# Moving 32 more tokens of a product-key expert layer from the dense path to row fetches

## The reference

```python
q = (xt @ w_query).reshape(NT, PEER_HEADS, 2, D_KEY // 2)      # 8 heads
s = jnp.einsum('nhpd,pkd->nhpk', q, sub_keys)                  # 2 x 128 keys
v1, i1 = lax.top_k(s[:, :, 0], 16); v2, i2 = lax.top_k(s[:, :, 1], 16)
cand = (v1[..., :, None] + v2[..., None, :]).reshape(NT, 8, 256)
best, ci = lax.top_k(cand, 16)
idx = e1 * N_KEYS + e2            # 8 x 16 = 128 experts of 16384 for a token
gate = jax.nn.softmax(best, axis=-1)
act = jax.nn.gelu(jnp.einsum('cd,ced->ce', xc, expert_u[ic]), approximate=False)
y = jnp.einsum('ce,ced->cd', gc * act, expert_v[ic])
```

## Time and profile before

| | |
|---|---|
| Runs | 4306.17 us median of 3 (4293.15 to 4307.22) |
| The profiled execution | 4302.8 us, of which its span is 4301.0 |
| PE, DVE, POOL, ACT busy | 4162.1, 2571.1, 2259.6, 1306.7 us |
| DMA | 832.09 MB, mean 193 GB/s |
| Gates, 48 units | from 2320.9 us of the span to 2770.9 |
| Rest, 40 units | to 3129.4 |
| Values, 128 units, and the last norm | to 4301.0 |

### The profile page before, as it was taken

How to read it: one execution, slowest core, us unless ns; L and a number is a source line. 1 busy time by engine, 2 the same in 40 slices (tenths; PEclk the granted TensorE clock), 3 DMA queues, 4 the chain that set the end, 5 groups by cost and what they waited for, 6 DMA issues and landing times.

```text
span 4301.0 us, 69877 instructions
## 1 busy us (share of the span) xinstructions
PE 4162.1 (97%) x27220; PEld 3743.0 (87%) x27220; DVE 2571.1 (60%) x3908; ACT 1306.7 (30%) x1265; POOL 2259.6 (53%) x866
## 2 busy tenths in 40 slices
PE   7999999999999999899999999999988999999998
PEld 5777777777788778799999999999978999999997
DVE  4344343444554542477775999745558777777775
ACT  4332322333322221233233444422222222222223
POOL 4333223233234344344445544567767778888884
PEclk9999999999999999999999999999999999999999
DMA  3222222222223442233334555499979989899983
GB/s 121 89 88 80 86 87 82 84 87 87 97 89 104 140 170 98 80 122 122 123 120 145 191 188 195 186 353 395 380 291 356 356 326 356 351 358 360 357 329 109
DMA packets 205230, 832.09 MB, mean 193 GB/s; under 512 B 15864, under 2 KB 98040, under 8 KB 120080
## 3 DMA queue, kind: packets, MB, share of 16 engines
q1 hardware_dynamic: 135024, 486.69, 31.5%
q0 software_dynamic: 36864, 268.45, 15.1%
q10 hardware_dynamic: 33184, 74.63, 4.5%
HBM read 760.99 MB, written 68.71 MB: 193 GB/s over the span
## 4 chain that ended last, share of the span: by engine, by line
PE 79%; issue 9%; POOL 4%; DVE 3%; DMA 3%; ACT 1%; SPq 0%; POOLq 0%; DVEq 0%; ACTq 0%
PE ps L348 17%; PE ps L350 16%; PE ps L349 16%; PE ps L1874 7%; PE ps L1875 7%; PE ps L1876 7%; POOL wl L343 4%; DMA raw<-stream 2%; PE ps L1578 2%; PE ps L1836 1%; ACT wh L339 1%; DVE rowb L1416 1%; DVE gal L1423 1%; PE ps L1730 0%; PE ps L1721 0%
## 5 line engine op out<-in xcount | busy, mean ns | idle before, releaser
L343 POOL TENSOR_TENSOR wl<-raw,wh 128x2048 fp32r<-128x2048 f32 x396 | 1839.0, 4644 | 1878.5 <-ACT wh L339 1878.0
L348 PE MATMUL ps<-xh,wh 128*128 128x384 f32 (+1 forms) x3904 | 1463.3, 375 | 43.4 <-POOL wl L343 22.2
L350 PE MATMUL ps<-xh,wl 128*128 128x384 f32 (+1 forms) x3904 | 1430.0, 366 | 0.0
L349 PE MATMUL ps<-xl,wh 128*128 128x384 f32 (+1 forms) x3904 | 1429.4, 366 | 0.0
L339 ACT ACTIVATE wh<-raw 128x2048 fp32r<-128x2048 f32 x396 | 759.0, 1917 | 1937.5 <-PE ps L350 1066.2
L348 PEld LDWEIGHTS ps<-xh,wh 128*128 128x128 f32 x3904 | 737.9, 189 | 140.4 <-issue 36.8
L350 PEld LDWEIGHTS ps<-xh,wl 128*128 128x128 f32 x3904 | 737.4, 189 | 83.4
L349 PEld LDWEIGHTS ps<-xl,wh 128*128 128x128 f32 x3904 | 738.1, 189 | 81.3 <-issue 7.7
L1874 PE MATMUL ps<-gah,wh 128*128 128x384 f32 x2048 | 699.7, 342 | 44.4 <-POOL wl L343 22.3
L1875 PE MATMUL ps<-gal,wh 128*128 128x384 f32 x2048 | 696.7, 340 | 0.0
L1876 PE MATMUL ps<-gah,wl 128*128 128x384 f32 x2048 | 696.1, 340 | 0.0
(11 more groups left out here) (321 smaller groups left out, 3700.6 us busy)
## 6 DMA issues: line engine op xcount, KB each, us to landing
raw<-stream SPq DMA_DIRECT2D x396, 1024.0 KB, 4.8
gelu_scratch<-preb ACTq DMA_DIRECT2D x128, 192.0 KB
gates_scratch<-stage ACTq DMA_DIRECT2D x12, 2048.0 KB, 6.5
gt<-gates_scratch SPq DMA_DIRECT2D x32, 768.0 KB
act<-gelu_scratch SPq DMA_DIRECT2D x32, 768.0 KB
mergegate_scratch<-sgb ACTq DMA_DIRECT2D x32, 256.0 KB, 2.1
sgm<-mergegate_scratch SPq DMA_DIRECT2D x32, 256.0 KB, 2.7
h_in<-x_t SPq DMA_DIRECT2D x4, 1024.0 KB, 8.8
```

What stands on the lines that cost most here:

```text
L343: pool.tensor_tensor(wl[s][:, :], raw[s][:, :], wh[s][:, :].bitcast(F32), ALU.subtract).then_inc(w_lo, 1)
L348: pe.matmul(dst, w_h, h[:, kx, lo:], start=start, stop=False)
L349: pe.matmul(dst, w_h, l[:, kx, lo:], start=False, stop=False)
L350: return pe.matmul(dst, w_l, h[:, kx, lo:], start=False, stop=stop)
```

## The change

G becomes 160 and N 352. The 32 new fetched tokens have 128 slots each as well; they are packed four slots to one DMA (32 tokens x 4 slots on 128 partitions), so 32 more fetches of u-rows and 32 of v-rows (`ALL` = 160). Their numbers and gates are brought onto the four quarters of the partitions by eight small DMAs (`idx_1`), their x stands four times in `xd`, and their sum is taken by a matmul with `sel`, which adds the quarters.

The fetches begin in the gates stage, from its fourth unit on: 12 by its twelfth unit, 116 to the third unit of the rest, then the 32 new ones up to group 3; v-rows 128 over groups 4 to 23 (1.6 to a unit) and 32 over groups 25 to 29. Since xg now holds banks 0 to 3 during the gates, these use one bank (6), two tokens at a time. H waits in DRAM (`h_scratch`) from the head routing to the end of the rest; its place holds xd and three row buffers. DVE writes only the plain one-hot (`ohp`), ACT multiplies it by the two gate halves (`act_scale`). The gates are 88 sets of four tokens: two sets with each of 12 score units (`GATES_TWO`), one with each of 64 (`GATES_ONE`); the rest has 12 units. `stage` holds 16 tokens (`GT`) instead of 32, so a group's gates come in pieces of 256 bytes. The group load stands behind the fourth unit's load instead of the second's. The sum of the first 128 tokens is taken after group 24, the other at the end.

```diff
@@ constants
-SC_HEAD, SC_TAIL, SC_EGT, OH = 4, 6, 2, 8
+SC_HEAD, SC_TAIL, SC_EGT, OH = 4, 6, 2, 4
-G = P
+G2 = 32
+SETS = P // G2
+G = P + G2
+ALL = SLOTS + SLOTS // SETS
+GATES_TWO = 12
+GATES_ONE = N // OH - 2 * GATES_TWO
-VALUE_FETCHES = [range(min(N_REST + 2 * k, SLOTS), min(N_REST + 2 * k + 2, SLOTS)) for k in range(V_FIRST)]
+fetches(0, 12, range(3, GATES_TWO), 0)
+fetches(12, SLOTS - 12, range(GATES_TWO, F_GATES + R_TURNED - 1), 0)
...
+fetches(ALL, SLOTS, range(at_group(V_GROUP) - 1, at_group(W_GROUP - 1) - 1), 0)
+fetches(ALL + SLOTS, ALL - SLOTS, range(at_group(W_GROUP) - 2, at_group(GROUPS - 3) + 1), at_group(W_GROUP))
-    GT = 32
+    h_d = dram("h_scratch", (4, P, D))
+    GT = 16
@@ load_values
-                    if c == 1 and ahead:
+                    if c == 3 and ahead:
@@ scalar
+            act.wait_ge(h_ready, KT)
+            for c in range(4):
+                act.dma_start(h_d[c], quarter_h(c)).then_inc(h_moved[c], 16)
+            def act_scale(k, c):
+                act.wait_ge(oh_plain, k + 1)
+                for u in range(OH):
+                    for m, gate in enumerate((gate_h[:, :].bitcast(F32), gate_l[:, :])):
+                        last = act.activation(oh1[:, OH * c + u, m, :], ohp[:, OH * c + u, :], ACT.Copy, scale=gate[:, bass.ds(OH * k + u, 1)])
+                last.then_inc(oh_ready, 1)
+            def act_upper(p, s, q):
+                act.wait_ge(oh_used, p + 1)
+                act.activation(of_tokens(s, q), gate_parts[:, :, 0, :], ACT.Copy).then_inc(dense_upper, 1)
@@ act_gates
-                    for c in range(2):
-                        act.wait_ge(oh_used, 2 * k + c + 1)
-                        act.activation(of_tokens(s, q, c), gate_parts(c)[:, :, 0, :], ACT.Copy).then_inc(dense_upper, 1)
+                        act_upper(2 * k, s, 2 * q)
+                        if not (last and q == GT // OH - 1):
+                            act_scale(k + 1, (q + 1) % 2)
+                        act_upper(2 * k + 1, s, 2 * q + 1)
+                if r == F_REST - 2:
+                    act.wait_ge(row_used, LAST_IN_H + 1)
+                    act.wait_ge(xg_ready, 2)
+                    for c in range(4):
+                        act.dma_start(quarter_h(c), h_d[c]).then_inc(h_moved[c], 16)
@@ vector
-                for u in range(4):
-                    for m, gate in enumerate((gate_h[:, :].bitcast(F32), gate_l[:, :])):
-                        last = dve.tensor_scalar(oh1[:, 4 * c + u, m, :], iota_ps, EGT[:, 0, bass.ds(at + u, 1)],
-                                                 gate[:, bass.ds(at + u, 1)], ALU.is_equal, ALU.mult)
+                dve.tensor_tensor(oh2[:, c:c + OH, :], numbers, spread(1), ALU.is_equal)
+                dve.tensor_tensor(ohp[:, c:c + OH, :], numbers, spread(0), ALU.is_equal).then_inc(oh_plain, 1)
+                for k in range(2 * j, 2 * j + 2) if j < GATES_TWO else range(GATES_TWO + j, GATES_TWO + j + 1):
+                    dense(2 * k)
+                    if k + 1 < N // OH:
+                        onehots(k + 1)
+                    if used and (j >= GATES_TWO or k % 2):
+                        use(used.pop(0))
+                    dense(2 * k + 1)
@@ tensor
+            def gates(k, c, h, first=False):
+                if not first:
+                    pe.wait_ge(dense_saved, 2 * k + h)
+                if h == 0:
+                    pe.wait_ge(oh_ready, k + 1)
+                for u in range(2):
+                    at = OH * c + 2 * h + u
+                    last = pe.matmul(bank(6)[:, 256 * u:256 * u + 256], oh2[:, at, :], oh1[:, at, :, :].rearrange("p m e -> p (m e)"), start=True, stop=True)
+                last.then_inc(oh_used, 1)
```

More of the change, by code:

```diff
@@ new lines, with fetches @@
+FETCHED_AT = {}
+def fetches(start, count, units, used_from):
+    for n in range(count):
+        j = units[len(units) * n // count]
+        FETCHED_AT[start + n] = j
+        FETCHED[j].append(start + n)
+        USED[max(j + 1, used_from)].append(start + n)
+at_group = lambda g: F_ALL + NC4 * g
+ROWS_LOW, ROWS = 2, 5
+J_BACK, J_HIGH = F_ALL - 3, F_ALL + 2
+fetches(0, 12, range(3, GATES_TWO), 0)
+fetches(12, SLOTS - 12, range(GATES_TWO, F_GATES + R_TURNED - 1), 0)
+fetches(SLOTS, 7, range(F_GATES + R_TURNED, J_BACK), F_GATES + R_TURNED + 1)
@@ L85 @@
+LAST_IN_H = max(n for n in range(2 * ALL) if FETCHED_AT[n] < J_BACK)
 R_GATED = F_REST - 5
@@ L997, in act_halves @@
+            for s in range(2):
+                act_gates(GB - 2 + s, s, 4, 4 * (GB - 2 + s) - GATES_TWO, last=s == 1)
             def act_halves(g, s, e):
@@ new lines, in score_parts, with gates_two, gates_one @@
+            def score_parts(e, s, n, of, between):
+                pe.wait_ge(pre_ready, e - 1)
+                for c in range(of):
+                    between(c)
+                    unit(pe, n, s, bank(4 + s)[:, 0:N], KT // of * c, KT // of * (c + 1), lo=G)
+            def gates_two(i, s, first=False):
+                score_parts(SC_GATES + i, s, score_unit(SC_GATES) + i, 4,
+                            lambda c: gates(2 * i + c // 2, c // 2, c % 2, first and c == 0))
+            def gates_one(i, s):
+                score_parts(SC_GATES + i, s, score_unit(SC_GATES) + i, 2, lambda c: gates(GATES_TWO + i, s, c))
@@ L1841, in _, with turn @@
+            def turn(value):
+                pe.wait_ge(sets_ready, value)
+                for k in range(KT):
+                    last = pe.transpose(bank(k // 4)[:, P * (k % 4):P * (k % 4) + P], xd[:, k, :], ident[:, :])
+                last.then_inc(xg_ready, 1)
             for s in range(2):
-                gates(s, s, first=s == 0)
-            with pe.Fori(1, N // OH // 2) as i:
+                gates_two(s, s, first=s == 0)
+            turn(3)
+            with pe.Fori(1, GATES_TWO // 2) as i:
@@ L1844, in _ @@
                 for s in range(2):
-                    gates(2 * i + s, s)
-            def rest(i):
+                    gates_two(2 * i + s, s)
+            with pe.Fori(GATES_TWO // 2, F_GATES // 2) as i:
                 for s in range(2):
-                    ahead(SC_REST + 2 * i + s, s, score_unit(SC_REST) + 2 * i + s)
-            for i in range(2):
-                rest(i)
-            pe.wait_ge(xd_ready, 1)
-            for k in range(KT):
-                last = pe.transpose(bank(k // 4)[:, P * (k % 4):P * (k % 4) + P], xd[:, k, :], ident[:, :])
@@ L1856, in _ @@
-            last.then_inc(xg_ready, 1)
-            with pe.Fori(2, F_REST // 2) as i:
-                rest(i)
+                    gates_one(2 * i + s, s)
+            for r in range(F_REST):
+                ahead(SC_REST + r, r % 2, score_unit(SC_REST) + r)
+                if r == R_TURNED:
+                    turn(4)
             def pe_values(g, s, first=False):
```

292 lines of the change are left out of this document (164 added, 128 removed).

## The result

The changed kernel took 4361.64 us (median of 4 runs, 4356.67 to 4371.66) against 4299.66 for the kernel before (4 runs beside it): ratio 1.0145, 95% interval 1.0125 to 1.0165. It is slower by 1.45%, clear of the noise. The forecast was 4298 us, no change; the result lies 64 us above it, inside the range of 4215 to 4385. The profiled execution has a span of 4362.8 us.

The account below looks back on a forecast made before the run. PE was taken to set the pace, with DMA close behind. From the profiled 4302.8 us, routing -27, gates and what follows +66 and values -44 gave 4298 us; the range for 8 in 10 was 4215 to 4385.

Parts of the forecast that it names:

- A narrower matmul: All matmul units: 352 columns take 0.162 us each, so a unit falls 0.68 us, 174 us over 256 units at most.
- Routing: Head routing, 40 units: PE-bound, so the whole 0.68 us a unit arrives, -27 us.
- The ring: Gates: PE, ACT and DVE steps in series, 7.1 us per four tokens; gates and what follows 874 us, +66.
- The clock: First 12 gate units: PE gaps of some 2.5 us leave its clock at 2.4 GHz, so nothing added.
- The values: Value stage: 8.4 us a unit, between 8.0 and 9.2, from DMA floor and late weight tiles; total -44 us.
- The DMA term: Value units: 3.09 MB at 392 to 396 GB/s, 7.8 to 7.9 us; with smaller gate pieces a floor of 8.0.
- The value groups stall as groups 2 to 6 did: Rival for the value units: DMA demand exceeds what PE leaves, 9.2 us a unit, +80, 4378 us; chance 0.20.
- small pieces: Rival for the value units: gate-tile transfers under 512 B take double time, +50, 4348 us; chance 0.07.
- The light end: Rival, gates and values: scaling at 1.7 us (-39) and value units at 8.0 (-40), 4219 us; chance 0.20.
- a ring that isn't one: Rival for the gates: DVE or ACT run ahead, units 8.7 and 8.25, 735 us instead of 874, total 4159; chance 0.05.
- The signs: Expected in the profile: matmuls 0.162 apart, gate units 16 and 9.1, scalings 0.30, value units 8.4 with DMA 0.95 or more.

Follow-up runs that it names:

- e4: Changed kernel with DVE making the next four tokens' plain one-hots ahead of the first addition in the gates: 4311.03 us, ratio 1.0024 to the kernel before.
- e5: e4's edit on the changed kernel, plus ACT's eight scalings split into two halves, each ahead of an upper copy: 4421.08 us, ratio 1.0261.
- e10: Changed kernel without DVE's gal subtractions from group 2 on, semaphore raised instead, old low halves reused: 4318.08 us, ratio 1.0026.
- e6: Changed kernel with a value unit's gal subtractions made at the next unit's start, ahead of its first addition to H: 4319.68 us, ratio 1.0027.
- e13: Changed kernel with GpSimd's row fetches in value units moved behind its gate multiplications, ahead of the next split: 4364.21 us, ratio 1.0120.
- e3: Changed kernel with DVE's adds of fetched v-rows taking 256 of 2048 columns, fetches whole: 4320.27 us, ratio 1.0042.
- e11: Changed kernel with the edits of e9 and e10 together, half value rows and no gal subtractions from group 2 on: 4238.62 us, ratio 0.9832.
- e9: Changed kernel fetching only half of each value row, DVE reading the half twice: 4348.94 us, ratio 1.0088.
- e2: Changed kernel with the gates' group load reading as many bytes in 1408 pieces of 512 bytes instead of 2816 of 256: 4345.92 us, ratio 1.0102.
- e14: e13's edit on a 4256.98 us version combining e4's and e6's edits with ACT's upper copies ahead of halved scalings: 4283.92 us, ratio 0.9942.

## Why the prediction was wrong, step by step

- **A narrower matmul**: right, 0.160 us for 0.162 foretold (eight started in 1.12 us, 3099.74 to 3100.86). **Routing**: -31 for -27.
- **The ring**: right. (ACT's terms in the one-set unit take add and broadcasts as 1.85, where the list above them gives 0.65 + 1.29 = 1.94; that is 0.05 us a unit.) A scaling follows the last after 0.29 to 0.30 us, the plain one-hots, the scalings and the copy come one after another as listed, and DVE's addition takes 610 ns for 0.65 foretold. By the Trainium skill (ScalarE: Activation LUTs, the paragraph on ACTIVATE's cost) a scaling should follow the last after an estimated 0.29 us; the trace agrees. The 12 units took 183 us for 192, the 64 took 590 for 582, the rest 107 for 93 + 7; together 879.7 for 874. e4 and e5 show that it is a ring: a step taken out of it or put into it moved the units.
- **The clock** in the 12 units: the stretch has 0.92. It cost nothing there that can be seen, as assumed, since the ring and not PE sets those units: PE was busy 0.68 (near 0.6 foretold), and 52.7 of its 58.1 us of idle time were waits for DVE's addition.
- **The values: the step that failed** is "I take 8.4 us a unit, between 8.0 and 9.2". It was 9.06 in the 80 units (+48 us against 677) and 9.30 in the 20 of groups 25 to 29 (+18 against 168); the first eight were 10.08 for 10.0 and the next eight 9.06 for 8.9. These come to 68 us; between -44 and +22 lie 66. The sum for a value unit weighed PE, DMA, the weight tile's burst and GpSimd, and left DVE out. DVE's own work would have fitted: four additions of 0.52, 1.6 rows of 2.35 and a subtraction of 0.52 are 6.4 us a unit. What was missing is that a subtraction with both inputs in SBUF waits out GpSimd's work, and that GpSimd lost the short pause in which it used to get in. In its place the runs show subtractions of 2.4 us on average between 3500 and 4000 us, additions to H queued behind them, and PE waiting 45.9 us of 500 for these. The prediction had the idea at hand: of the first `xd` it says that it can be held up by POOL, but it didn't ask that of the subtractions. e10, e6 and e13 show the hold and what it costs. The lost pause is read from the traces of the two kernels, in the counts above; that it went because the unit got shorter is argued, and no run tried it by itself.
- The DMA term was too low as well: without DVE's wait the unit is 8.6, not 8.4 (e3, e6, e10), and 7.80 with half rows (e11). With it corrected alone the forecast would have been some 20 us higher, an estimate from 0.2 us over 100 units.
- **The rivals.** "The value groups stall as groups 2 to 6 did" came nearest in the unit (9.2). In time it (4378) and small pieces (4348) lie about as near to 4361.64. Its condition, from 8.6 a unit, was met; but its mechanism, demand on DMA, was only the lower of two limits, as e9 shows. Small pieces: 16 us, not 50; and the sentence that before all pieces were 512 B or more holds of the gate tile only, as the page of the kernel before counts 15864 packets under 512 B. Here the Trainium skill (DMA: Bandwidth & Descriptors, the table at its head) speaks of read-modify-write under 512 B. These are reads from DRAM of 256 B, and the traces of the changed kernel and e2 differ by 0.1 us a unit, with DVE's wait in place; that doesn't bear out a doubled time. The light end and a ring that isn't one are out: the scalings took 0.30 each and the value units 9.06, and the two kinds of gate unit 15.23 and 9.22.
- The signs that were to show it: DMA share 0.95 at 8.4 us a unit was foretold, 0.89 came with 9.06. That alone doesn't clear DMA: e13 and e14 have 0.90 and 0.88 with units of 9.0, and there ACT's splits waited 26 and 25 times for weight tiles that came late.

How much of the 9.06 is PE's lower clock was not separated: the stretch has 0.96, and the stretch of 8.45 us a unit had 1.00, which by an estimate is at most 0.04 of 724 us, 29 us. From 3500 to 4000 us the changed kernel has 0.97 with PE idle for 51 us, and e11 0.99 with PE idle for 10.

## What to carry to other kernels

When a change shortens the bounding engine's unit, write the sum for every engine again, DVE too, and look for pauses that another engine was using. A row whose mean is well above that of its equals tells of a wait inside the instruction: in the kernel before, a subtraction took 1197 ns on average (959 between 3500 and 4000 us) beside an addition, as wide, of 553.

```profile
L1423 DVE TENSOR_TENSOR gal<-act,gah 128x384 fp32r<-128x384 f32 x128 | 150.5, 1197 | 1.4 <-ACT gah L999 1.4
L1433 DVE TENSOR_TENSOR H<-ps,H 128x384 f32<-128x384 f32 x512 | 277.8, 553 | 320.3 <-PE ps L1876 317.5 <-DVE sum L1478 0.5
```

One experiment that gives nothing doesn't clear a suspect: half the row traffic gave 0.12 us alone and 0.79 once DVE was out of the way. A ring over three engines is judged by what stands between its steps: moving the one-hots out of it gave 51 us, and four scalings put ahead of its copy cost 110.
